# A 32-expert layer whose weight stream changes from 2 MB to 4 MB transfers, and what that does to the matrix engine's reads

## The chip, the cores and the metric

One core of one Trainium2 chip runs the whole program. The time is the device time of one execution in microseconds. The kernel before took 1160.23 us (median of 3 runs, 1159.47 to 1162.91). The profiled execution took 1164.89 us, of which 1163.1 us lie between its first and its last instruction (its span).

## The reference, cut to what matters

A decoder layer on 256 tokens of width 1024, all in float32: a norm, one input projection, a sparse-attention group and a delta-rule group, an output projection with residual, then a norm and a mixture of 32 experts of which each token uses 4. The change lies in the experts:

```python
def expert_ffn(xb, wg, bg, wu, bu, wd, bd):
    gate = jnp.minimum(xb @ wg + bg, SWIGLU_LIMIT)
    up = jnp.clip(xb @ wu + bu, -SWIGLU_LIMIT, SWIGLU_LIMIT)
    glu = gate * jax.nn.sigmoid(gate * SWIGLU_ALPHA)
    return ((up + 1.0) * glu) @ wd + bd
...
top_val, top_idx = lax.top_k(h @ w_router + b_router, 4)
gates = jax.nn.softmax(top_val, axis=-1)
# every expert is applied to the tokens that chose it, weighted by its gate, summed over experts
```

Each expert has three 1024 x 1024 matrices (gate, up, down) of 4 MB; the 96 matrices are 402.7 MB, and all of them are read once.

## The kernel before, in words

The front (attention, delta rule, router) takes about the first 233 us. The rest is a loop over 16 pairs of experts in `pair`, which every engine has its own version of. Up to 64 tokens (`CAP`) are gathered per expert by a matmul with a selection matrix (L928), turned (L937), multiplied with gate and up (`stream`, L964), put through the SwiGLU on the vector and scalar engines (L1765 to L1774), turned (L992), multiplied with down (L964 again), and each pair's result is scattered back onto the tokens by a matmul (L1004) and added to `x` (L1786). Because only 64 rows are live, two matmuls that write the two halves of PSUM's partitions (columns 0 to 511 and 512 to 1023 of the result) stand side by side; each program matmul is two instructions in the trace.

Weights arrive in halves of a matrix. A half is 2 MB, 16 KB in each of 128 partitions, and fills one of ten slots (`SLOTS`). Half `j` goes to slot `EXPERT_RING[j % 10]`; the order of the ring is that in which the front gives the slots up. Half `h` of a matrix holds the rows `h*512 + 4*p + c` in partition `p` (L408), so that four neighbouring rows are one run of memory. SyncE issues them in order in `chunks` (L497 to L502): it waits until the slot's previous half has been used (`freed`), then starts the DMA, whose end raises `landed`. TensorE waits for `landed` in front of each half and raises `freed` behind it. The last half comes in four pieces (`last_chunk`, L504) so that work on it can begin early.

Since row `4*p + c` sits in partition `p`, the other operand has to be in the same order. ACT (L1248) and POOL (L1386) therefore write the normalised tokens `h2` column by column in that order (`rows_of_runs`, `place_of_runs`), and DVE writes `m_act` so (L1774).

In the text below, "the first half of the up matrix of a pair's second expert" is the half with `j % 12 == 8`, since a pair of experts has 12 halves.

Of the kernel before, what the change touches and what calls it, by code (L numbers as in the profile page):

```python
# [24 lines left out]
ALU = mybir.AluOpType  # L25
AX = mybir.AxisListType

P = 128
# [7 lines left out]
NE = 32  # L36
CAP = 64
ROUNDS = SEQ // CAP
FRONT_SLOTS = 4
SLOTS = 10  # L40
PAIRS = NE // 2
BODY = 5
LAPS = 6
TURNS = (PAIRS - 1) // BODY
CHUNKS = 12
# [5 lines left out]
C_ID = 0  # L51
C_IO = C_ID + P
C_ONE = C_IO + CAP
# [41 lines left out]
REGIONS = {"qk_turned": 4, "attention": 5, "inverse": 6, "scan": 7, "turned_input": 8, "tables": 9}  # L95


EXPERT_RING = [3, 0, 4, 5, 7, 1, 6, 2, 8, 9]
assert len(EXPERT_RING) == SLOTS and CHUNKS * BODY == SLOTS * LAPS and 1 + BODY * TURNS == PAIRS

# [76 lines left out]
def hybrid_block(nc, a, out):  # L177
    slab, front_uses, front_landed = slab_plan()
# [8 lines left out]
    with ctx:  # L187
        def sb(name, cols, dt=F32):
            return ctx.enter_context(nc.sbuf_tensor(name, [P, cols], dt))
# [13 lines left out]
        nsa = sb("nsa", 8192 + 2048)  # L203
        rB = nsa[:, 8192:]
        late = {8: nsa[:, 6144:]}

        tables = sb("tables", C_ONE + 4096)
        late[9] = tables[:, C_ONE:]
        cst = tables[:, 0:C_END]
# [7 lines left out]
        def at(name, lo, n):  # L217
            return ring[:, REGIONS[name] * 4096 + lo:REGIONS[name] * 4096 + lo + n]

# [14 lines left out]

        ident = cst[:, C_ID:C_ID + P]
# [122 lines left out]
        def ringv(s):  # L358
            return late[s] if s in late else ring[:, s * 4096:(s + 1) * 4096]

# [23 lines left out]
        def chunk(r, turn, j):  # L384

            k = j % SLOTS
            s = EXPERT_RING[k]
            lap = r * ((6 * NE + SLOTS - 1 - k) // SLOTS) + turn * LAPS + j // SLOTS  # L390
            return s, lap + front_uses[s], lap * 16 + (front_landed[s] + 16)

        def used(eng, r, turn, j):
# [13 lines left out]

        wexp = [a[n][0].rearrange("e (h p c) f -> e h p (c f)", h=2, p=P)  # L408
                for n in ("exp_w_gate", "exp_w_up", "exp_w_down")]

        def rows_of_runs(v):
            return v.rearrange("p (h q c) -> p h c q", h=2, c=4)

# [7 lines left out]
        def _(sp):  # L421
# [34 lines left out]
            sp.dma_start(xt[:, 1, :], xi[1]).then_inc(sem("x1_landed"), 16)  # L456
            sp.dma_start(cst[:, 0:C_ONE], a["const_table"][:, 0:C_ONE]).then_inc(sem("ident_landed"), 16)
            load("c")
# [38 lines left out]

            def chunks(r, turn, lo, hi):
                for j in range(lo, hi):
                    s, uses, _ = chunk(r, turn, j)  # L500
                    sp.wait_ge(freed[s], uses)
                    sp.dma_start(ringv(s), wexp[j % 6 // 2][turn * (2 * BODY) + j // 6, j % 2]).then_inc(landed[s], 16)  # L502

            def last_chunk():  # L504

                s, uses, _ = chunk(0, TURNS - 1, CHUNKS * (BODY + 1) - 1)
                sp.wait_ge(freed[s], uses)
                for c in range(4):
                    sp.dma_start(ringv(s)[:, 1024 * c:1024 * c + 1024], wexp[2][NE - 1, 1][:, 1024 * c:1024 * c + 1024])\
                        .then_inc(landed[s] if c == 3 else sem(f"piece_landed{c}"), 16)  # L510
# [27 lines left out]
        def _(pe):  # L538
# [393 lines left out]
            def turn_rows(m, first=False):  # L932
# [5 lines left out]
                i.then_inc(sem("rows_turned"), 1)  # L938

            def biases(buf):  # L940

                for fh in range(2):
                    for w, o in enumerate((bG, bU)):
                        rows = slice(NE * (w + 1), NE * (w + 2))
                        pe.matmul(o[64 * fh:64 * fh + 64, :], m_eb[buf][rows, :], btab[rows, 512 * fh:512 * fh + 512],  # L945
                                  start=True, stop=False, skip_group_check=True)

            def stream(o, r, turn, j0, lhs, opens=False, pieces=False):

                for j in (j0, j0 + 1):  # L950
                    s, _, val = chunk(r, turn, j)
                    apart = pieces and j > j0
                    if not apart:
                        pe.wait_ge(landed[s], val)
                    w = ringv(s).rearrange("p (c f) -> p c f", c=4)
                    for c in range(4):
                        if apart and c < 3:
                            pe.wait_ge(sem(f"piece_landed{c}"), 16)
                        elif apart:
                            pe.wait_ge(landed[s], val)  # L960
                        cc = (j - j0) * 4 + c
                        lt = lhs[:, (cc % 4) * P + (cc // 4) * CAP:(cc % 4) * P + (cc // 4) * CAP + CAP]
                        for fh in range(2):
                            i = pe.matmul(o[64 * fh:64 * fh + 64, :], lt, w[:, c, 512 * fh:512 * fh + 512],  # L964
                                          start=(opens and cc == 0), stop=(cc == 7), skip_group_check=True)
                            if fh == 1 and c == 3:
                                i.then_inc(freed[s], 1)
                return i

            def pair(r, turn, i, opens=False, last=False):  # L970
                it = r * PAIRS + turn * BODY + i
                j0 = CHUNKS * i
                for par in range(2):
# [5 lines left out]
                    for w, o in enumerate((bG, bU)):  # L979
                        stream(o, r, turn, j0 + 6 * par + 2 * w, m_hT[par])  # L980
                    gather(1 - par, m + 1)
# [409 lines left out]
        def _(dve):  # L1391
            nchain = [0]
            V = nc.vector
# [345 lines left out]

            iota = cst[:, C_IO:C_IO + CAP]  # L1740

            def select(buf, e):

                for t in range(T2):
                    ins = V.tensor_scalar(m_sel[buf][:, t, :], iota, posm[:, t, bass.ds(e, 1)], None, ALU.is_equal)  # L1745
                ins.then_inc(sem("sel_ready"), 1)
                V.tensor_tensor(m_eb[buf], bcast(cst[:, bass.ds(e + (C_ID + NE), 1)], [P, CAP]),
                                bcast(cst[:, bass.ds(e + (C_ID + 2 * NE), 1)], [P, CAP]), ALU.add)\
                    .then_inc(sem("eb_ready"), 1)
# [119 lines left out]
```

## Time and profile before

| | |
|---|---|
| median of 3 runs | 1160.23 us (1159.47 to 1162.91) |
| profiled execution | 1164.89 us, span 1163.1 us |
| TensorE busy | 1089.6 us, 94% |
| VectorE, ScalarE, GpSimd busy | 321.6, 213.2, 38.9 us |
| DMA moved | 430.93 MB in 46585 packets |
| DMA, from 262 us to 1134 us | 425 to 429 GB/s in every slice |
| mean granted TensorE clock | 0.988 |

The page cuts the span into 40 slices of 29 us and gives each engine's busy share in tenths, the granted clock, and what the DMA engines moved. A long busy time says that an engine is used, not that it sets the end: the chain of work that ended last, and who waits for whom, tell that.

### The profile page before, as it was taken

Reading aid. Unit: us, or ns where it says so; the run is one execution under the profiler, and the core shown is the slowest. Engines: PE = TensorE matmul, PEld = TensorE weight load, DVE = VectorE, ACT = ScalarE, POOL = GpSimd, SP = SyncE. Lnnn points to the kernel's source line nnn. Section 1 sums busy time; section 2 is a strip of 40 time slices with the busy share of each in tenths; the row PEclk is TensorE's granted clock in tenths of the full one; section 3 lists DMA queues with packets and bytes.
Section 4 is the critical chain, followed back from the end, with each engine's and each line's share of the span. In section 5 each row is a group of like instructions: output and inputs, shape, how many; then the busy total and the mean of one; then the engine's idle time right before and its main releaser. Section 6 shows DMA issues by size and latency. Waiting matters only on the chain.

```text
span 1163.1 us, 12735 instructions
## 1 busy us (share of the span) xinstructions
PE 1089.6 (94%) x5122; PEld 447.1 (38%) x5122; DVE 321.6 (28%) x660; ACT 213.2 (18%) x410; POOL 38.9 (3%) x43
## 2 busy tenths in 40 slices
PE   6999999899999999999899999989898999999986
PEld 4577587533333333333233333323232333333332
DVE  2377745321212222121212221212121212121221
ACT  3246753311111110101011101110101010101010
POOL 0001240100000000000000000000000000000000
PEclk9999999879999999999999999999999999999999
DMA  9724245779999999999999999999999999999994
GB/s 330 254 89 128 91 163 191 298 288 428 428 426 429 426 429 428 428 426 429 425 428 428 427 427 428 427 428 428 427 429 428 428 427 429 428 427 428 428 426 162
DMA packets 46585, 430.93 MB, mean 371 GB/s; under 512 B 7556, under 2 KB 13148, under 8 KB 22076
## 3 DMA queue, kind: packets, MB, share of 16 engines
q1 hardware_dynamic: 46524, 430.06, 89.2%
q8 instruction: 45, 0.74, 0.3%
q14 instruction: 16, 0.13, 0.0%
HBM read 429.00 MB, written 1.05 MB: 370 GB/s over the span
## 4 chain that ended last, share of the span: by engine, by line
PE 65%; DMA 24%; DVE 4%; ACT 3%; issue 2%; SPq 1%; DVEq 0%; ACTq 0%
PE bank L964 42%; DMA ring<-in_exp_w_up_dram 15%; DMA tables<-in_exp_w_up_dram 8%; PE bank L1004 3%; PE bank L584 3%; PE bank L571 3%; PE bank L601 3%; ACT nsa L1046 3%; PE bank L841 2%; PE bank L945 2%; PE bank L928 2%; DVE nsa L1774 1%; PE bank L592 1%; DVE nsa L1770 1%; PE bank L992 1%
## 5 line engine op out<-in xcount | busy, mean ns | idle before, releaser
L964 PE MATMUL bank<-ring,nsa 128*64 128x512 f32 x2464 | 547.7, 598 | 19.7 <-DMA ring<-in_exp_w_up_dram 9.9
L964 PEld LDWEIGHTS bank<-ring,nsa 128*64 128x64 f32 x2464 | 172.5, 138 | 376.5 <-issue 339.0
L1046 ACT ACTIVATE nsa<-bank 128x512 f32<-128x512 f32 (+6 forms) x187 | 95.2, 543 | 506.3 <-PE bank L928 254.0
L1779 DVE COPY nsa<-bank 64x512 f32<-64x512 f32 x32 | 22.2, 694 | 273.9 <-PE bank L964 273.9
L1765 DVE TENSOR_SCALAR nsa<-bank 128x512 f32<-128x512 f32 x32 | 22.1, 692 | 239.3 <-PE bank L964 239.3
L1043 ACT ACTIVATE nsa<-nsa 128x512 f32<-128x512 f32 (+2 forms) x35 | 21.1, 607 | 345.5 <-DVE nsa L1765 345.5
L964 PE MATMUL bank<-nsa 128*64 128x512 f32 x304 | 69.2, 597 | 3.9 <-DMA nsa<-in_exp_w_up_dram 2.5
L964 PE MATMUL bank<-tables,nsa 128*64 128x512 f32 x304 | 68.6, 593 | 3.6 <-DMA tables<-in_exp_w_up_dram 2.5
L1004 PE MATMUL bank<-nsa 128*128 128x512 f32 x128 | 59.5, 604 | 12.5 <-ACT nsa L1046 12.5
L1770 DVE TENSOR_SCALAR nsa<-bank 128x512 f32<-128x512 f32 x32 | 22.1, 692 | 170.7 <-PE bank L964 170.7
L928 PE MATMUL bank<-rA,nsa 128*64 128x512 f32 x264 | 64.0, 607 | 0.9 <-DVE nsa L1745 0.9
L1786 DVE TENSOR_TENSOR x<-x,bank 128x512 f32<-128x512 f32 x64 | 44.0, 688 | 31.7 <-PE bank L1004 25.3
L571 PE MATMUL bank<-ring,nsa 128*128 128x512 f32 (+1 forms) x128 | 50.0, 547 | 0.0
L584 PE MATMUL bank<-nsa,ring 128*128 128x256 f32 x192 | 42.4, 379 | 0.0
L1004 PEld LDWEIGHTS bank<-nsa 128*128 128x128 f32 x128 | 22.8, 189 | 49.9 <-issue 49.9
L964 PEld LDWEIGHTS bank<-tables,nsa 128*64 128x64 f32 x304 | 21.6, 137 | 48.0 <-issue 41.1
L964 PEld LDWEIGHTS bank<-nsa 128*64 128x64 f32 x304 | 20.8, 137 | 47.3 <-issue 40.2
L945 PE MATMUL bank<-btab,nsa 32*64 32x512 f32 x256 | 35.8, 629 | 3.1 <-issue 3.1
L584 PEld LDWEIGHTS bank<-nsa,ring 128*128 128x128 f32 x192 | 36.2, 190 | 5.2 <-issue 0.5
L1046 ACT ACTIVATE ring<-bank 128x512 f32<-128x512 f32 (+3 forms) x54 | 29.8, 589 | 40.7 <-PE bank L601 15.4
L1774 DVE SCALAR_TENSOR_TENSOR nsa<-nsa 128x512 f32<-128x512 f32 x32 | 33.9, 1058 | 3.3
L928 PEld LDWEIGHTS bank<-rA,nsa 128*64 128x64 f32 x264 | 19.2, 139 | 38.8 <-issue 38.8
(196 smaller groups left out, 650.6 us busy)
## 6 DMA issues: line engine op xcount, KB each, us to landing
ring<-in_exp_w_gate_dram SPq DMA_DIRECT2D x52, 2048.0 KB, 36.2
ring<-in_exp_w_down_dram SPq DMA_DIRECT2D x51, 2048.0 KB, 34.7
ring<-in_exp_w_up_dram SPq DMA_DIRECT2D x50, 2048.0 KB, 36.9
nsa<-in_exp_w_up_dram SPq DMA_DIRECT2D x7, 2048.0 KB, 35.5
tables<-in_exp_w_up_dram SPq DMA_DIRECT2D x7, 2048.0 KB, 37.0
ring<-in_w_in_dram SPq DMA_DIRECT2D x6, 2048.0 KB, 11.6
nsa<-in_exp_w_gate_dram SPq DMA_DIRECT2D x6, 2048.0 KB, 37.8
tables<-in_exp_w_gate_dram SPq DMA_DIRECT2D x6, 2048.0 KB, 39.3
```

Of the source, the lines that this page charges most:

```text
L571: m = pe.matmul(o[:, 0:n], hT[:, c, t * P:(t + 1) * P], w[:, c, 0:n], start=(c == 0), stop=(c == KC - 1))
L584: m = pe.matmul(o[:, u * SEQ:(u + 1) * SEQ], w[:, c, mc0:mc0 + P], hT[:, c, :], start=(c == 0), stop=(c == KC - 1))
L601: m = pe.matmul(o[:, hd * P:(hd + 1) * P], lhs[i][:, hd, :], rhs[i][:, hd, :], start=(i == 0), stop=(i == n - 1))
L841: m = pe.matmul(o[:, :], mixT[:, lo + k, t * P:(t + 1) * P], w[:, k, n * 512:(n + 1) * 512], start=(k == 0), stop=(k == 3))
L928: i = pe.matmul(bA[64 * hf:64 * hf + 64, :], m_sel[buf][:, t, :], h2[:, t, 512 * hf:512 * hf + 512], start=(t == 0), stop=(t == 1), skip_g ...
L945: pe.matmul(o[64 * fh:64 * fh + 64, :], m_eb[buf][rows, :], btab[rows, 512 * fh:512 * fh + 512], start=True, stop=False, skip_group_check= ...
L964: i = pe.matmul(o[64 * fh:64 * fh + 64, :], lt, w[:, c, 512 * fh:512 * fh + 512], start=(opens and cc == 0), stop=(cc == 7), skip_group_ch ...
L1004: i = pe.matmul(scatter_bank[hf][t][:, :], m_selwT[:, t, :], m_y[:, 512 * hf:512 * hf + 512], start=True, stop=not opens)
L1046: return nc.scalar.activation(o, i, ACT.Copy)
L1770: V.tensor_scalar(m_uc, bU[:, :], -7.0, 7.0, ALU.max, ALU.min).then_inc(sem("up_read"), 1)
L1774: V.scalar_tensor_tensor(out=m_act.rearrange("p (c q) -> p q c", c=4), in0=m_uc.rearrange("p (q c) -> p q c", c=4), scalar=1.0, in1=m_gs.r ...
L1786: V.tensor_tensor(xs, xs, scatter_bank[hf][t][:, :], ALU.add).then_inc(sem("added"), 1)
```

## The change

The memory layout of a matrix in SBUF changes: partition `p` now holds the rows `8*p` to `8*p + 7`, which are one run of 32 KB, and half `h` of the matrix is rows `8*p + 4*h + c`. From half 24 on, a matrix is fetched by one DMA into two slots, which for that are laid side by side in SBUF (`PLACE` puts the ring's slots in ring order, slots 8 and 9 both lie in `nsa` now). The first 24 halves (4 experts) and the last 6 (the last expert) still come one by one, the very last in four pieces. The DMA waits until the second of its two slots is free; TensorE waits for the whole matrix in front of its first half and not again in front of its second.

For the down matrix to find its rows in that order, the columns of gate and up are taken in the same order: the matmul that made columns 0 to 511 now makes those whose number has `(n // 4) % 2 == 0`, the other one the rest. It reads runs of 4 floats, 8 floats apart (`in_runs`). The bias rows are read likewise. The constants that the expert loop needs (identity, counting row) move to a buffer of their own, `marks`.

```diff
-        wexp = [a[n][0].rearrange("e (h p c) f -> e h p (c f)", h=2, p=P)
+        wexp = [a[n][0].rearrange("e (p h c) f -> e h p (c f)", h=2, p=P)
...
+        whole = [a[n][0].rearrange("e (p r) f -> e p (r f)", p=P) for n in ("exp_w_gate", "exp_w_up", "exp_w_down")]
...
-            return v.rearrange("p (h q c) -> p h c q", h=2, c=4)
+            return v.rearrange("p (q h c) -> p h c q", h=2, c=4)
...
+            def chunks(r, turn, lo, hi):
+                for j in range(lo, hi, 2):
+                    s, uses, _ = chunk(r, turn, j + 1)
+                    sp.wait_ge(freed[s], uses)
+                    s = chunk(r, turn, j)[0]
+                    sp.dma_start(pairv(s), whole[j % 6 // 2][turn * (2 * BODY) + j // 6]).then_inc(landed[s], 16)
...
-            chunks(0, 0, 0, CHUNKS)
-            with sp.Fori(0, TURNS - 1) as turn:
+            halves(0, 0, 0, SINGLY)
+            chunks(0, 0, SINGLY, CHUNKS * (BODY + 1))
+            for turn in range(1, TURNS - 1):
                 chunks(0, turn, CHUNKS, CHUNKS * (BODY + 1))
-            chunks(0, TURNS - 1, CHUNKS, CHUNKS * (BODY + 1) - 1)
+            chunks(0, TURNS - 1, CHUNKS, CHUNKS * (BODY + 1) - 6)
+            halves(0, TURNS - 1, CHUNKS * (BODY + 1) - 6, CHUNKS * (BODY + 1) - 1)
...
+            def in_runs(w, fh):
+                return w.rearrange("p (q h c) -> p h q c", h=2, c=4)[:, fh]
...
-                    if not apart:
+                    if j == j0:
                         pe.wait_ge(landed[s], val)
+                    elif j < SINGLY or pieces and not apart:
+                        pe.wait_ge(landed[s], second_half(j))
...
-                            i = pe.matmul(o[64 * fh:64 * fh + 64, :], lt, w[:, c, 512 * fh:512 * fh + 512],
+                            wc = w[:, c, 512 * fh:512 * fh + 512] if o is bD else in_runs(w[:, c, :], fh)
+                            i = pe.matmul(o[64 * fh:64 * fh + 64, :], lt, wc,
```

(`halves` is the old `chunks`.) On SyncE, where the fifth expert's weights begin (half 24), the order before is this; 128x4096 is a half, and the ISA rows compute register values of the loop:

```order
L502 DMA ring<-in_exp_w_down_dram 128x4096 x2
L502 ISA
L502 DMA ring<-in_exp_w_gate_dram 128x4096
L502 ISA
L502 DMA ring<-in_exp_w_gate_dram 128x4096
L502 DMA ring<-in_exp_w_up_dram 128x4096 x2
L502 DMA nsa<-in_exp_w_down_dram 128x4096
L502 DMA tables<-in_exp_w_down_dram 128x4096
```

The same place of the change, 128x8192 being a whole matrix:

```order
L518 DMA ring<-in_exp_w_down_dram 128x4096 x2
L527 DMA ring<-in_exp_w_gate_dram 128x8192
L527 DMA ring<-in_exp_w_up_dram 128x8192
L527 DMA nsa<-in_exp_w_down_dram 128x8192
L527 DMA ring<-in_exp_w_gate_dram 128x8192
```

Two DMAs became one, and nothing changed its place among the matrices. The end of the stream, where the last expert begins, stands so before:

```order
L502 DMA ring<-in_exp_w_down_dram 128x4096 x2
L502 DMA ring<-in_exp_w_gate_dram 128x4096 x2
L502 DMA nsa<-in_exp_w_up_dram 128x4096
L502 DMA tables<-in_exp_w_up_dram 128x4096
L502 DMA ring<-in_exp_w_down_dram 128x4096
L509 DMA ring<-in_exp_w_down_dram 128x1024 x4
```

and so after:

```order
L527 DMA ring<-in_exp_w_down_dram 128x8192
L518 DMA ring<-in_exp_w_gate_dram 128x4096 x2
L518 DMA nsa<-in_exp_w_up_dram 128x4096 x2
L518 DMA ring<-in_exp_w_down_dram 128x4096
L534 DMA ring<-in_exp_w_down_dram 128x1024 x4
```

Here only the down matrix of expert 30 is joined; the last six halves stand as they did. The rows of TensorE, VectorE, ScalarE and GpSimd keep their kind, number and place; only source lines and buffer names differ.

## Rows read from the trace of the kernel before

**Rows 1.** The page: TensorE's busy time, and GB/s of the 40 slices.
```profile
PE 1089.6 (94%) x5122; PEld 447.1 (38%) x5122; DVE 321.6 (28%) x660; ACT 213.2 (18%) x410; POOL 38.9 (3%) x43
...
GB/s 330 254 89 128 91 163 191 298 288 428 428 426 429 426 429 428 428 426 429 425 428 428 427 427 428 427 428 428 427 429 428 428 427 429 428 427 428 428 426 162
```
**Rows 2.** Windows: busy us (count) of PE, PEld, DVE, ACT, POOL; clock; DMA share; GB/s.
```profile
300.00:400.00 100.00, 97.78 (x464) 33.55 (x462) 20.08 (x39) 11.59 (x21) 0.00 (x0) 1.00 1.01 428
...
1000.00:1100.00 100.00, 91.73 (x422) 30.10 (x420) 20.84 (x41) 9.59 (x17) 0.00 (x0) 1.00 1.01 428
```
**Rows 3.** The chain that ended last, 296 to 353 us: start, us, what.
```profile
297.11 1.02 PE bank L945 x8
298.13 13.88 PE bank L964 x64
...
352.20 1.00 PE bank L945 x5
```
**Rows 4.** The same chain, 560 us to the end.
```profile
782.91 3.68 PE bank L964 x16
...
1092.22 45.62 DMA tables<-in_exp_w_up_dram
...
1137.88 3.68 PE bank L964 x16
...
1156.41 0.69 DVE x L1786
```
**Rows 5.** Waits: engine, line, waited for: us in total, times, longest.
```profile
SPq L502 <- PE bank L964: 785.0, 181, 13.8
...
PEld bank L964 <- DMA ring<-in_exp_w_up_dram: 19.4, 15, 2.1
```
**Rows 6.** DMA queues (packets, MB, share): 900:1100, 135:139, 22:24, 91:94 us.
```profile
DMA packets 5870, 85.54 MB, mean 428 GB/s; under 512 B 649, under 2 KB 649, under 8 KB 649
...
q1 hardware_dynamic: 5863, 85.43, 100.4%
...
q8 instruction: 7, 0.11, 0.2%
...
q1 hardware_dynamic: 406, 1.66, 101.2%
...
q1 hardware_dynamic: 379, 0.78, 105.4%
...
q1 hardware_dynamic: 1070, 1.10, 108.6%
```
**Rows 7.** The half issued between 310 and 313 us (half 25): KB, us to landing.
```profile
ring<-in_exp_w_gate_dram SPq DMA_DIRECT2D x1, 2048.0 KB, 17.3
```
**Rows 8.** Timeline, 220 to 252 us: start, us, instruction, idle before and releaser.
```profile
221.50 1.06 ACT L1043 ACTIVATE rA<-x 128x1024 f32<-128x1024 f32 x1 [1.05 <-DVE x L1685]
...
224.26 0.29 DVE L1705 TENSOR_TENSOR_SCAN st<-tables,st 128x32 f32<-128x32 f32 x1
...
225.72 2.12 ACT L1248 ACTIVATE rA<-x,st 128x1024 f32<-128x1024 f32 x1 [0.30 <-DVE st L1419]
...
227.99 2.87 POOL L1386 TENSOR_TENSOR rA<-rA,nsa 128x1024 f32<-128x1024 f32 x1 [4.14 <-ACT rA L1248]
...
228.40 2.54 DVE L1705 TENSOR_TENSOR_SCAN st<-tables,st 128x32 f32<-128x32 f32 x1
```
**Rows 9.** The page's costliest groups: busy us, mean ns | idle before, releaser.
```profile
L964 PE MATMUL bank<-ring,nsa 128*64 128x512 f32 x2464 | 547.7, 598 | 19.7 <-DMA ring<-in_exp_w_up_dram 9.9
...
L1765 DVE TENSOR_SCALAR nsa<-bank 128x512 f32<-128x512 f32 x32 | 22.1, 692 | 239.3 <-PE bank L964 239.3
...
L1774 DVE SCALAR_TENSOR_TENSOR nsa<-nsa 128x512 f32<-128x512 f32 x32 | 33.9, 1058 | 3.3
```
**Rows 10.** Timeline, 568 to 592 us: TensorE at the loop's turn.
```profile
575.64 1.24 PE L945 MATMUL bank<-btab,nsa 32*64 32x512 f32 x8 [3.06 <-issue]
```
**Rows 11.** Windows, 576 to 580 us, columns as in Rows 2.
```profile
576.00:580.00 4.00, 4.00 (x16) 1.01 (x10) 0.00 (x0) 0.00 (x0) 0.00 (x0) 0.57 1.01 426
```

More of the change, by code:

```diff
@@ L43 @@
 LAPS = 6
+SINGLY = 24
 TURNS = (PAIRS - 1) // BODY
@@ L98 @@
 EXPERT_RING = [3, 0, 4, 5, 7, 1, 6, 2, 8, 9]
+PLACE = {s: k for k, s in enumerate(EXPERT_RING[:8])}
 assert len(EXPERT_RING) == SLOTS and CHUNKS * BODY == SLOTS * LAPS and 1 + BODY * TURNS == PAIRS
@@ L202, in hybrid_block @@
         rA = sb("rA", 2048)
[L203 to L208, printed above, removed]
+        nsa = sb("nsa", 8192 + 2048 + 4096)
+        rB = nsa[:, 8192:10240]
+        late = {8: nsa[:, 6144:10240], 9: nsa[:, 10240:]}
+        marks = sb("marks", C_ONE)
+        tables = nsa[:, 10240 - C_ONE:]
         cst = tables[:, 0:C_END]
@@ L217, in at @@
         def at(name, lo, n):
-            return ring[:, REGIONS[name] * 4096 + lo:REGIONS[name] * 4096 + lo + n]
+            return ring[:, PLACE[REGIONS[name]] * 4096 + lo:PLACE[REGIONS[name]] * 4096 + lo + n]
         rD = at("qk_turned", 0, 3072)
@@ L233, in hybrid_block @@
         gain2 = nsa[:, 0:1024]
-        ident = cst[:, C_ID:C_ID + P]
+        ident = marks[:, C_ID:C_ID + P]
         ones = cst[:, C_ONE:C_ONE + P]
@@ L358, in ringv, with pairv @@
         def ringv(s):
-            return late[s] if s in late else ring[:, s * 4096:(s + 1) * 4096]
+            return late[s] if s in late else ring[:, PLACE[s] * 4096:(PLACE[s] + 1) * 4096]
+        def pairv(s):
+            return nsa[:, 6144:] if s in late else ring[:, PLACE[s] * 4096:(PLACE[s] + 2) * 4096]
         def signal_of(job):
@@ L391, in chunk, with second_half @@
             return s, lap + front_uses[s], lap * 16 + (front_landed[s] + 16)
+        def second_half(j):
+            k = j % SLOTS
+            s = EXPERT_RING[k]
+            n = j // SLOTS + 1 if j < SINGLY else len([i for i in range(SINGLY) if i % SLOTS == k]) + 1
+            return front_landed[s] + 16 * n
         def used(eng, r, turn, j):
@@ L456, in _ @@
             sp.dma_start(xt[:, 1, :], xi[1]).then_inc(sem("x1_landed"), 16)
-            sp.dma_start(cst[:, 0:C_ONE], a["const_table"][:, 0:C_ONE]).then_inc(sem("ident_landed"), 16)
+            sp.dma_start(marks[:, :], a["const_table"][:, 0:C_ONE]).then_inc(sem("ident_landed"), 16)
             load("c")
@@ L496, in _, with halves @@
             sp.dma_start(gain2, a["ffn_norm_g"][0].partition_broadcast(P)).then_inc(sem("gain2_landed"), 16)
-            def chunks(r, turn, lo, hi):
+            def halves(r, turn, lo, hi):
                 for j in range(lo, hi):
@@ L509, in last_chunk @@
                     sp.dma_start(ringv(s)[:, 1024 * c:1024 * c + 1024], wexp[2][NE - 1, 1][:, 1024 * c:1024 * c + 1024])\
-                        .then_inc(landed[s] if c == 3 else sem(f"piece_landed{c}"), 16)
-            chunks(0, 0, 0, CHUNKS)
-            with sp.Fori(0, TURNS - 1) as turn:
+                        .then_inc(sem(f"piece_landed{c}"), 16)
+            halves(0, 0, 0, SINGLY)
+            chunks(0, 0, SINGLY, CHUNKS * (BODY + 1))
+            for turn in range(1, TURNS - 1):
                 chunks(0, turn, CHUNKS, CHUNKS * (BODY + 1))
-            chunks(0, TURNS - 1, CHUNKS, CHUNKS * (BODY + 1) - 1)
+            chunks(0, TURNS - 1, CHUNKS, CHUNKS * (BODY + 1) - 6)
+            halves(0, TURNS - 1, CHUNKS * (BODY + 1) - 6, CHUNKS * (BODY + 1) - 1)
             last_chunk()
@@ L944, in biases @@
                         rows = slice(NE * (w + 1), NE * (w + 2))
-                        pe.matmul(o[64 * fh:64 * fh + 64, :], m_eb[buf][rows, :], btab[rows, 512 * fh:512 * fh + 512],
+                        pe.matmul(o[64 * fh:64 * fh + 64, :], m_eb[buf][rows, :], in_runs(btab[rows, :], fh),
                                   start=True, stop=False, skip_group_check=True)
@@ L951, in stream @@
                     s, _, val = chunk(r, turn, j)
-                    apart = pieces and j > j0
-                    if not apart:
+                    apart = pieces and j == CHUNKS * (BODY + 1) - 1
+                    if j == j0:
                         pe.wait_ge(landed[s], val)
+                    elif j < SINGLY or pieces and not apart:
+                        pe.wait_ge(landed[s], second_half(j))
                     w = ringv(s).rearrange("p (c f) -> p c f", c=4)
                     for c in range(4):
-                        if apart and c < 3:
+                        if apart:
                             pe.wait_ge(sem(f"piece_landed{c}"), 16)
-                        elif apart:
-                            pe.wait_ge(landed[s], val)
                         cc = (j - j0) * 4 + c
@@ L979, in pair @@
                     for w, o in enumerate((bG, bU)):
-                        stream(o, r, turn, j0 + 6 * par + 2 * w, m_hT[par])
+                        stream(o, r, turn, j0 + 6 * par + 2 * w, m_hT[par], pieces=(last and par == 1))
                     gather(1 - par, m + 1)
@@ L1738, in _ @@
                                         scalar=1.0, in1=chosen, op0=ALU.add, op1=ALU.mult))
-            iota = cst[:, C_IO:C_IO + CAP]
+            iota = marks[:, C_IO:C_IO + CAP]
             def select(buf, e):
@@ L1746, in select @@
                 ins.then_inc(sem("sel_ready"), 1)
-                V.tensor_tensor(m_eb[buf], bcast(cst[:, bass.ds(e + (C_ID + NE), 1)], [P, CAP]),
-                                bcast(cst[:, bass.ds(e + (C_ID + 2 * NE), 1)], [P, CAP]), ALU.add)\
+                V.tensor_tensor(m_eb[buf], bcast(marks[:, bass.ds(e + (C_ID + NE), 1)], [P, CAP]),
+                                bcast(marks[:, bass.ds(e + (C_ID + 2 * NE), 1)], [P, CAP]), ALU.add)\
                     .then_inc(sem("eb_ready"), 1)
```

## The prediction

> **What bounds the kernel now.** I read the page first. TensorE is busy for 94% of the span, which makes it look like the bound, but GB/s stands at 425 to 429 in thirty slices in a row, from about 260 us almost to the end [rows 1]. Two things that are both nearly full need a second view. The windows say which one has room: the DMA share is 1.01 early and late, while TensorE's busy time falls from 97.78 to 91.73 us in 100 [rows 2]. TensorE has gaps, the DMA engines have none.
>
> The chain of waits says the same in periods. Early, one pair of experts follows the last after 352.20 - 297.11 = 55.09 us without any DMA in the chain [rows 3]: that is what TensorE and its helpers need by themselves. Late, the chain passes through the landing of the last half of a pair's up matrices; six pairs take 1137.88 - 782.91 = 354.97 us, 59.16 us each [rows 4], or 4.93 us per half. Without the weights TensorE would be done at 297.11 + 15 x 55.09 + 3.1 (the turn of its loop, [rows 10]) + 6.7 (from 1156.41 to the end of the span, [rows 4]) = 1133.3 us, 30 us ahead of the real end. SyncE's long waits for TensorE [rows 5] are no contradiction: ten slots are full of transfers that are under way (45.62 us from issue to landing late in the run, [rows 4]), so nine halves queue in front of the engines. So the time is the start of the stream, plus 402.7 MB at the stream's rate, plus some 25 us of work after the last landings. Only the stream's rate, its start and that tail can move the end.
>
> **The change: packets.** The DMA engines handle a run of memory as one packet. Between 900 and 1100 us, 85.43 MB are 5214 packets of 16 KB; the other 649 are the tiny ones that tell a semaphore, one to eight packets of data [rows 6]. A full queue gives the time of a packet as engine time over packets, 16 engines times the stretch: 1 KB packets (91 to 94 us) 48/1070 = 44.9 ns, 2 KB (22 to 24 us) 32/379 = 84.4 ns, 4 KB (135 to 139 us) 64/406 = 157.6 ns, and 16 KB (3200 - 8.7)/5214 = 612.1 ns, where 8.7 us are charged to the small packets and the code fetch [rows 6]. Were all of it bytes, four times 157.6 would be 630. The line from the 4 KB row to 16 KB has 37.9 ns per KB and leaves 6.1 ns that do not depend on size; from the 2 KB row it is 9.0, from the 1 KB row 7.1. I take 7.1, the middle one, and keep 6.1 and 9.0.
>
> Halves 24 to 185 come as 81 whole matrices. Each saves, on every engine, eight packets of data and one small one: 9 x 7.1 = 64 ns, and 81 x 64 ns = 5.2 us (4.4 to 6.6). A 32 KB packet is in no row; below, the saving is bounded by nothing at all (a packet cut back to 16 KB), above by the nearest rows' 9.0 ns.
>
> The DMA page of the Trainium skill (DMA: Bandwidth & Descriptors, Why small descriptors are slow) speaks against this size: it puts a fixed cost of about 3 cycles beside one per 32 bytes on each packet, which is 0.6% of 16 KB. By that estimate halving the packets saves 0.3% of 81 matrices, 2.3 us, and not 5.2. The 16 KB and 4 KB rows show more than that per packet, so my sum goes by them.
>
> **The change: waits.** A joint DMA starts when its second slot is free, one half later than its first half did. That matters only if the queue runs dry. At its thinnest, where the joint ones begin, half 25 was issued behind half 24 and landed after 17.3 us [rows 7]; two halves of 4.93 leave 7.4 us that were ahead of both. The joint DMA goes out at that same moment, so the queue stays full: cost nothing. If it did run dry, every us of it would be lost.
>
> TensorE now waits for whole matrices. Per pair of experts it has about 59.16 - 0.38 - 55.09 = 3.7 us to spare; before, this came in small waits (longest 2.1 us, [rows 5]), now most of it falls together in front of one up matrix. In the middle the stream hides that. What counts is the last one, half 176 of expert 29: from its landing TensorE needs 55.09 us to the same place of the next pair, and one half (13.88/4 = 3.47 us, [rows 3]) until it stands before half 189. The stream needs 12 halves less four joint savings, 59.16 - 0.26 = 58.9 us. 58.6 against 58.9: just hidden, with 0.3 us left where there were over three before. I charge 0.3 us for it. After 189 nothing changes: halves 190 and 191 come singly and in pieces as they did.
>
> **The change: reading in runs.** Of each expert, 64 instructions of gate and up (13.88 us, [rows 3]) and the bias rows now read 4 floats and skip 4. No row shows TensorE reading like that. The nearest are of other engines: ACT takes 1.06 us over 1024 neighbouring floats and 2.12 us when it reads every fourth one [rows 8]; on DVE the step that writes its columns far apart takes 1058 ns beside 692 [rows 9]. Below I set no gain, since the columns are as many; above stand the factors 1.53 and 2.0. I take no cost, because those rows touch one float in each 16 bytes and this read uses every float of the 16 bytes it touches, as the contiguous read does.
>
> The skill has a rule for that (Advanced Engine Details and Errata, SBUF Cachelines): lines of 16 bytes, full speed from two hits on a line. With four hits it would be free, so the rule's sum is mine; by the ACT row's factor alone it would be hundreds of us. The ACT row agrees with the rule's other half.
>
> A small slowing would be hidden anyhow: gate and up are 32 x 13.88 = 444 us, TensorE's own end lies 1158.2 - 1133.3 = 24.9 us before the new one (1158.2 comes out of the sum below), and 24.9/444 is 5.6%.
>
> **The change: the rest.** In the front, ACT L1248 and POOL L1386 read every eighth float instead of every fourth. They already pay for a new 16 bytes with each float; I take no cost, at most once more their 2.12 and 2.87 us, which would reach the expert loop's start because DVE's scan beside POOL took 2.54 instead of 0.29 us [rows 8]. The unrolled loop on SyncE, `marks` and the new places of slots cost nothing: SyncE only waits.
>
> **Sum.** 5.2 - 0.3 = 4.9 us off the stream's end: the profiled execution's 1164.89 becomes 1160.0, its span 1158.2. The median of the runs lies 4.66 us below the profiled time, so 1160.23 - 4.9 = 1155.3 us.
>
> **Rivals.**
> 1. *Bytes, not packets, set the rate.* If the constant is a property of small packets only, or if 32 KB runs are cut back to 16 KB, what is left is at most the small packets, 81 x 7.1 ns = 0.6 us, less the 0.3: 1159.9. For it: the step from 1 KB to 2 KB to 4 KB to 16 KB isn't quite straight (39.5, 36.6, 37.9 ns per KB out of the four numbers above). Against it: three rows give 6 to 9 ns. The skill's 3 cycles would land between, at 1158.2.
> 2. *Skipping reads slow the matmuls* (the slower side). From 5.6% on, TensorE sets the end and each further percent costs 4.4 us. With DVE's 1.53: 0.53 x 444 - 24.9 = 210 us, 1366; with 10%, 19.5 us, 1175. For it: ACT's and DVE's rows. Against it: every 16 bytes are still used whole.
> 3. *The pooled wait drops the clock.* After 3.06 us without work at the loop's turn [rows 10], the granted clock over the next 4 us was 0.57, so part of it ran at 1.2 GHz instead of 2.4 [rows 11]. Waits of about 3 us now come once a pair. In the middle this is hidden (1.5 us against 3.7); in front of half 189 it isn't: 1.5 us minus what is already charged, about 1156.5.
> 4. *The stream speeds up more,* each KB at the 36.6 ns between the 2 KB and 4 KB rows: 16 KB in 586 instead of 606 ns is 3.4% of 81 matrices (81 x 9.86 = 799 us), 27 us. With the 5.2 that is more than TensorE can follow, and the end goes to TensorE's own, 29.8 us sooner: 1130.4. For it there is only that one pair of rows.
>
> **How the numbers follow.** What a measurement of this kernel tells from no change is about 0.3%, 3.5 us: faster means below 1156.75. Forecast (5.2 us minus at most about 2 of the tail): 0.58, of it 0.50 faster and 0.08 same. Rival 1: 0.15, 0.13 same. Rival 3: 0.10, half and half. Rival 2: 0.13, slower. Rival 4: 0.04. Together faster 0.61, same 0.26, slower 0.13. The range takes in the forecast with 6.6 us saved and some us of luck in the rate, and rival 1 with a us of spread: 1151 to 1161. Rivals 2 and 4 are left out.
>
> **What would show it.** Right: 81 x 16 x 9 = 11,664 packets fewer than 46585, GB/s at 430 to 431 in the full slices, six pairs at 58.8 us each, waits for up matrices of about 3 us, the same mean for L964's matmuls (598 ns), DVE's and POOL's rows of the front unchanged. Packets at 16 KB or GB/s at 428 mean rival 1; a longer L964 and a period above 58.8 without DMA in the chain mean rival 2; a mean clock under 0.98 means rival 3. Holes in GB/s after 310 us would mean that the late start of joint DMAs, which I set at nothing, is what counts.

## The result and the profile after

The changed kernel takes 1155.17 us (median of 5 runs, 1153.3 to 1158.5), the one before 1161.03 us (5 runs, 1159.47 to 1162.91). The ratio is 0.9938, 95% interval 0.9922 to 0.9955: 0.6% faster. The forecast was 1155.3.

The page after, against [rows 1]: the busy time of each engine, GB/s of the 40 slices, and the packets of the whole run.

```profile
PE 1087.9 (94%) x5122; PEld 450.3 (39%) x5122; DVE 321.7 (28%) x660; ACT 212.9 (18%) x410; POOL 38.9 (3%) x43
...
GB/s 334 255 90 124 96 165 177 289 336 430 434 426 435 433 427 432 433 430 427 434 430 428 432 434 430 429 432 430 430 432 431 430 430 434 429 430 432 434 419 161
DMA packets 34919, 430.91 MB, mean 374 GB/s; under 512 B 6260, under 2 KB 11852, under 8 KB 20780
```

The full slices moved from about 428 to about 431 GB/s. There are 46585 - 34919 = 11,666 packets fewer. No engine's busy time moved by more than 3.2 us. The same two windows as [rows 2] (busy us of PE, PEld, DVE, ACT, POOL; clock; DMA share; GB/s):

```profile
300.00:400.00 100.00, 97.15 (x462) 33.12 (x456) 20.66 (x40) 12.16 (x22) 0.00 (x0) 1.00 1.01 432
1000.00:1100.00 100.00, 92.78 (x430) 31.61 (x430) 22.36 (x46) 10.21 (x18) 0.00 (x0) 1.00 1.00 430
```

The DMA engines are still full and TensorE still has gaps late in the run: the bound is the same and has moved a little. The queue from 900 to 1100 us, against [rows 6]:

```profile
DMA packets 2959, 86.12 MB, mean 431 GB/s; under 512 B 328, under 2 KB 328, under 8 KB 328
...
q1 hardware_dynamic: 2953, 86.02, 100.0%
```

86.02 MB in 2953 - 328 = 2625 packets are 32 KB each: the long runs are kept whole. The costliest group, against [rows 9] (busy us, mean ns | idle before):

```profile
L996 PE MATMUL bank<-ring,nsa 128*64 128x512 f32 x2464 | 544.4, 597 | 15.9 <-DMA ring<-in_exp_w_up_dram 8.1
```

L996 is the line that was L964. Its matmuls, two thirds of which now read in runs of four floats, take 597 ns where they took 598. The early chain against [rows 3] (start, us, what):

```profile
293.70 1.02 PE bank L976 x8
294.72 13.88 PE bank L996 x64
...
348.80 1.02 PE bank L976 x8
```

The period is 348.80 - 293.70 = 55.10 us, against 55.09 before. The late chain, against [rows 4]:

```profile
735.91 39.34 DMA ring<-in_exp_w_up_dram
...
1027.44 40.73 DMA ring<-in_exp_w_up_dram
...
1068.22 7.11 PE bank L996 x32
...
1085.74 42.34 DMA nsa<-in_exp_w_up_dram
1128.12 3.68 PE bank L996 x16
...
1142.94 3.69 PE bank L1036 x8
1146.65 0.69 DVE x L1818
```

From the landing at 735.91 + 39.34 = 775.25 to the one at 1027.44 + 40.73 = 1068.17 are five pairs: 58.58 us each. The same five pairs of the kernel before end with this landing, at 1078.10, and start at 782.87, which is 59.05 us each:

```profile
1033.48 44.62 DMA ring<-in_exp_w_up_dram
```

The sixth pair, up to half 189, takes longer in both, 59.91 and 59.74 us, so that six pairs take 58.80 us each where there were 59.16. TensorE now starts a whole matrix (x32) behind the landing, and only at the end, behind half 189, half of one (x16) as before.

**Which part of the difference is the change.** The two profiled executions differ by 1163.1 - 1153.4 = 9.7 us, the medians by 5.9. SyncE's rows show a part of it that has nothing to do with the change. They show the issue of half 10, the first DMA that waits for the expert loop; first of the kernel before, then of the changed one:

```profile
246.72 3.76 SPq L502 DMA_DIRECT2D ring<-in_exp_w_down_dram  x2
```

```profile
243.32 3.76 SPq L518 DMA_DIRECT2D ring<-in_exp_w_down_dram  x2
```

3.4 of the 9.7 us were there before the first joint DMA. Windows of TensorE around that time, before and then after:

```profile
238.00:242.00 4.00, 4.00 (x16) 1.35 (x17) 0.00 (x0) 1.88 (x2) 0.00 (x0) 0.50 0.33 139
242.00:246.00 4.00, 4.00 (x12) 1.09 (x10) 0.00 (x0) 0.00 (x0) 0.00 (x0) 0.58 0.00 0
```

```profile
234.00:238.00 4.00, 3.33 (x8) 0.53 (x4) 1.78 (x8) 0.60 (x1) 0.00 (x0) 0.60 0.91 360
238.00:242.00 4.00, 3.98 (x24) 1.54 (x26) 0.00 (x0) 1.88 (x2) 0.00 (x0) 1.00 0.31 131
```

TensorE ran at 1.2 GHz until about 245 us in the one execution and until about 237 us in the other, so the expert loop's first matmuls were slow in one and not in the other. E10 below shows that this moves between executions of one program. So I compare profiled executions from the issue of half 10 on. From there to the landing of half 189 the kernel before takes 1137.84 - 246.72 = 891.12 us and the changed one 1128.08 - 243.32 = 884.76: 6.4 us less. That, and not 9.7, is the change.

### The profile page after: what moved, and what is told of

It is laid out like the page before. It is cut to its first block, busy times and chain, and to the rows that moved or that the text cites. A ratio compares the mean times of both kernels' runs of the same rounds, so it can differ in the third digit from the quotient of the medians.

```text
span 1153.4 us, 12445 instructions
## 1 busy us (share of the span) xinstructions
PE 1087.9 (94%) x5122; PEld 450.3 (39%) x5122; DVE 321.7 (28%) x660; ACT 212.9 (18%) x410; POOL 38.9 (3%) x43
## 2 busy tenths in 40 slices
DMA packets 34919, 430.91 MB, mean 374 GB/s; under 512 B 6260, under 2 KB 11852, under 8 KB 20780
## 3 DMA queue, kind: packets, MB, share of 16 engines
HBM read 429.00 MB, written 1.05 MB: 373 GB/s over the span
## 4 chain that ended last, share of the span: by engine, by line
PE 68%; DMA 22%; DVE 5%; ACT 3%; issue 1%; SPq 0%; DVEq 0%; ACTq 0%
PE bank L996 44%; DMA ring<-in_exp_w_up_dram 14%; DMA nsa<-in_exp_w_up_dram 7%; PE bank L598 4%; PE bank L1036 3%; PE bank L611 3%; PE bank L628 3%; ACT nsa L1078 2%; PE bank L868 2%; PE bank L976 2%; PE bank L955 2%; DVE nsa L1806 1%; PE bank L619 1%; PE bank L1024 1%; DVE nsa L1802 1%
## 5 line engine op out<-in xcount | busy, mean ns | idle before, releaser
L996 PE MATMUL bank<-ring,nsa 128*64 128x512 f32 x2464 | 544.4, 597 | 15.9 <-DMA ring<-in_exp_w_up_dram 8.1
L996 PEld LDWEIGHTS bank<-ring,nsa 128*64 128x64 f32 x2464 | 174.3, 137 | 367.6 <-issue 345.5
L996 PE MATMUL bank<-nsa 128*64 128x512 f32 x608 | 136.3, 601 | 4.9 <-DMA nsa<-in_exp_w_up_dram 3.5
L996 PEld LDWEIGHTS bank<-nsa 128*64 128x64 f32 x608 | 42.8, 138 | 93.1 <-issue 84.6
L1036 PE MATMUL bank<-nsa 128*128 128x512 f32 x128 | 59.5, 604 | 12.5 <-ACT nsa L1078 12.5
L1036 PEld LDWEIGHTS bank<-nsa 128*128 128x128 f32 x128 | 22.7, 189 | 49.9 <-issue 49.9
L1078 ACT ACTIVATE ring<-bank 128x512 f32<-128x512 f32 (+3 forms) x54 | 29.8, 589 | 39.8 <-PE bank L628 15.4
L598 PEld LDWEIGHTS bank<-ring,nsa 128*128 128x128 f32 x128 | 24.8, 197 | 23.1 <-issue 21.0
```

The lines of the kernel that those rows point to most:

```text
L598: m = pe.matmul(o[:, 0:n], hT[:, c, t * P:(t + 1) * P], w[:, c, 0:n], start=(c == 0), stop=(c == KC - 1))
L996: i = pe.matmul(o[64 * fh:64 * fh + 64, :], lt, wc, start=(opens and cc == 0), stop=(cc == 7), skip_group_check=True)
L1036: i = pe.matmul(scatter_bank[hf][t][:, :], m_selwT[:, t, :], m_y[:, 512 * hf:512 * hf + 512], start=True, stop=not opens)
L1078: return nc.scalar.activation(o, i, ACT.Copy)
```

## The experiments

Each ratio is to the kernel before, in runs of the same chip. "Stream" is the time from the issue of half 10 to the landing of half 189, "to the end" that from the same issue to the start of the last group of matmuls of L1004 or L1036 (before: 1152.70 - 246.72 = 905.98; after: 1142.94 - 243.32 = 899.62). The row of before:

```profile
1152.70 3.69 PE bank L1004 x8
```

**E1, the runs alone.** The new split of the rows and the reads in runs, in the kernel before; halves still come singly.

```diff
-        wexp = [a[n][0].rearrange("e (h p c) f -> e h p (c f)", h=2, p=P)
+        wexp = [a[n][0].rearrange("e (p h c) f -> e h p (c f)", h=2, p=P)
...
+            wc = w[:, c, 512 * fh:512 * fh + 512] if o is bD else in_runs(w[:, c, :], fh)
```

> The kernel before with the new layout alone: halves in order (p h c), gate, up and bias rows read in runs of 4 floats, every half still fetched by its own DMA (16 KB packets, 2 MB). Packet theory (each packet costs about 7 ns beside its bytes): nothing in the stream changes, so the time is that of before within 1.5 us (about 1161), and 16 KB packets stay at about 612 ns of engine time. Rival A, the skipping read costs TensorE something: L964's matmuls above 598 ns and a pair period above 55.09 us in the part that TensorE sets. Rival B, the layout itself (memory order, 32 KB between partitions) makes the stream faster: about 1155, GB/s above 428.

Measured: 1163.75 us (12 runs) against 1162.93 (23), ratio 1.0005 (0.9993 to 1.0016); stream 890.97. The reads in runs cost nothing: its chain has the row below, the same to 0.01 us as the contiguous read.

```profile
923.40 13.88 PE bank L969 x64
```

**E2, joint DMAs of 16 KB runs.** The changed kernel, slots, pooled waits, unrolled loop and all, but with the old split of the rows, so that one DMA brings two runs of 16 KB per partition; reads are contiguous.

```diff
-    whole = [a[n][0].rearrange("e (p r) f -> e p (r f)", p=P) ...
+    whole = [a[n][0].rearrange("e (h p r) f -> e p h (r f)", h=2, p=P) ...
-    sp.dma_start(pairv(s), whole[...][...])
+    sp.dma_start(pairv(s).rearrange("p (h r) -> p h r", h=2), whole[...][...])
```

> The changed kernel with the old order of rows and contiguous column reads: whole matrices by one DMA into two neighbouring slots, but as two runs of 16 KB in each partition. Same waits and same number of DMAs as the changed kernel, packets as before (about 46,600 less 81 x 16 small ones). Packet theory: only the small packets go, 0.6 us, minus 0.3 us of tail, so about 1160.5, the time of before within 1.5 us. Rival C, joint DMAs as such (fewer issues and completions) bring the gain: about 1155. Rival D, whole-matrix waits cost something that the changed kernel's packets hide: above 1162.5.

Measured: 1162.75 us (12 runs), ratio 1.0008 (0.9995 to 1.002); stream 891.53. Its queue between 900 and 1100 us:

```profile
DMA packets 5548, 85.53 MB, mean 428 GB/s; under 512 B 328, under 2 KB 328, under 8 KB 328
```

As many small packets as in the changed kernel (328), but data in 16 KB packets and the old rate. So fewer DMAs, fewer semaphore packets and fewer waits are worth nothing; the gain is in the length of the runs. Rival 1's remnant, 0.6 us from small packets, isn't there either: from 320 to 1100 us E2 moves 332.98 MB with 1272 small packets, the kernel before 333.00 MB with 2540.

**E3, runs of 8 KB.** The kernel before with each half brought by two DMAs.

```diff
-   sp.dma_start(ringv(s), wexp[...][...]).then_inc(landed[s], 16)
+   for u in range(2):
+       sp.dma_start(ringv(s)[:, 2048 * u:2048 * u + 2048],
+                    wexp[...][...][:, 2048 * u:2048 * u + 2048]).then_inc(landed[s], 16)
```

> The kernel before with every half fetched by two DMAs of 8 KB runs (1 MB each) instead of one of 16 KB runs; waits as before. This doubles the suspected cost. Packet theory: per half and engine 8 more data packets and 1 more small one, 9 x 7.1 = 64 ns, for the 180 halves from half 10 on 11.5 us: 1172.5 (6.1 ns: 1171, 9.0 ns: 1175.6), GB/s about 423. Rival 1 of the prediction (bytes alone set the rate at these sizes): at most 180 x 7 ns = 1.3 us, about 1162.

Measured: 1175.06 us (4 runs), ratio 1.0103 (1.0084 to 1.0122): 12 us slower, the mirror of the change and larger: 180 halves by 8 are 1440 more data packets, where the change took away 648. Its stream takes 904.40 us, 13.28 more than before, or 9.2 ns for each. The queue from 320 to 1100 us of before, of the changed kernel, and of E3:

```profile
q1 hardware_dynamic: 22864, 333.00, 100.4%
```

```profile
q1 hardware_dynamic: 11514, 335.35, 100.0%
```

```profile
q1 hardware_dynamic: 45025, 327.86, 101.1%
```

780 us by 16 engines are 12,480 us. Over the data packets, by their megabytes 40,022, 20,325 and 10,234, that is 311.8 ns for 8 KB, 614.0 ns for 16 KB and 1219.5 ns for 32 KB, the small packets' share included. Two of 8 KB cost 9.6 ns more than one of 16 KB, two of 16 KB 8.6 ns more than one of 32 KB.

**E4 and E5, extra matmuls before the expert loop.** The late rise of the clock costs some 3 us, so I tried to keep TensorE busy in the router's wait: two more matmuls in E4, six smaller ones (32 rows instead of 128) in E5, some of them around the gather (their results are overwritten by the work that follows).

```diff
+            def keep_busy(n):
+                for _ in range(n):
+                    pe.matmul(bS1[:, :], ident, gain2[:, 0:512], start=True, stop=True)
...
+            keep_busy(2)
```

> The changed kernel with two extra matmuls (128x512, results never used, into a free bank) placed where TensorE waits for the router's choice, just ahead of the expert loop. In the profile of before the clock was granted at half for 20.5 us around the loop's start, in that of after for 13.7 us, and half 10 (the start of the stream) was issued 3.4 us earlier in the latter. Clock theory: with TensorE kept busy the half-clock stretch ends sooner, half 10 goes out up to 3 us before the changed kernel's 243.3 us, and the time falls by as much: 1152 to 1154. Rival: the stretch is set by what went before, nothing changes, or the extra matmuls delay the gather: 1155 to 1158.

> The changed kernel with six extra matmuls (results never used): three in the wait for the router's choice, one before the gather, one after it, one after the turn, all ahead of the expert loop. Two such matmuls (e4) changed nothing in the clock. Clock theory: with the gaps around the gather filled too, full clock comes back before 240 us, half 10 goes out before 243 us, and the time is 1150 to 1153. Rival: they only delay the gather by 1 to 3 us and the stretch stays, 1156 to 1160.

Measured: E4 1156.45 us (6 runs), ratio 0.9942 (0.9922 to 0.9963), no different from the change itself. E5 1160.24 us (12 runs), ratio 0.9979 (0.9966 to 0.9992), worse by some 4 us than the change. E4's matmuls filled only the router's wait, and the clock stayed low until about 245 us. E5 left TensorE no gap from 226 us on, and the clock still came back only for part of the time around 240 us, fell again, and half 10 went out at 248.42 us, later than in any other profiled execution. Windows of E4, then of E5:

```profile
238.00:242.00 4.00, 4.00 (x14) 0.77 (x8) 0.00 (x0) 1.68 (x2) 0.00 (x0) 0.50 0.00 0
242.00:246.00 4.00, 4.00 (x14) 1.22 (x12) 0.00 (x0) 0.00 (x0) 0.00 (x0) 0.63 0.00 0
```

```profile
234.00:238.00 4.00, 4.00 (x8) 1.12 (x10) 2.85 (x14) 0.00 (x0) 0.00 (x0) 0.50 0.77 262
238.00:242.00 4.00, 4.00 (x12) 1.00 (x8) 0.00 (x0) 1.47 (x3) 0.00 (x0) 0.85 0.61 262
242.00:246.00 4.00, 4.00 (x15) 0.97 (x16) 0.00 (x0) 1.01 (x1) 0.00 (x0) 0.58 0.00 0
```

My theory of a cheap warming fell in both forms. Behind the loop's start E5 is the change: its stream takes 884.68 us.

**E6 and E7, reads with real strides.** To see what TensorE pays for skipping when the 16 bytes are not used whole. Gate and up read other floats of the same slots, so that the output is not the layer's: E6 one float in each 32 bytes, E7 every second float.

```diff
-  wc = ... else in_runs(w[:, c, :], fh)
+  wc = ... else ringv(s).rearrange("p (q k) -> p k q", k=8)[:, 2 * c + fh]      # E6
+  wc = ... else w[:, c, :].rearrange("p (q h) -> p h q", h=2)[:, fh]            # E7
```

> The changed kernel, but gate and up read every eighth float of the slot (one float in each 32 bytes, 512 columns as before; it reads parts of the slot that belong to other columns, so the output is not the layer's). This is the read that ACT's row of before paid double for. Theory (what counts is how much of each 16 bytes is used, which is nothing for TensorE at four floats of four): L996's mean rises from 598 ns, by up to a factor of 2 for gate and up, TensorE then sets the end at 1155 + up to 420 us. Rival: TensorE doesn't mind any stride of float32 columns, time as after, about 1156.

> The changed kernel, but gate and up read every second float of a row (two floats in each 16 bytes; columns go to other places, so the output is not the layer's). If one float in 32 bytes costs TensorE something and two in 16 bytes nothing, a full-speed limit lies between; if e6 costs nothing, neither does this: about 1156 us, L996 at 598 ns. If the cost goes by 16-byte pieces per column, it lies at half of e6's.

Measured, one run each: E6 1637.86 us, E7 1161.18. The 64 matmuls of gate and up in E6's chain and in E7's:

```profile
325.21 29.51 PE bank L997 x64
```

```profile
297.73 14.55 PE bank L997 x64
```

Runs of four floats 13.88, every second float 14.55 (1.05 times), lone floats 29.51 (2.13 times). Every second float adds 32 x 0.67 = 21.4 us, more than all of the room: E7's late chain has no DMA in it, TensorE sets its end, and from the issue of half 10 (245.07) to the last group of matmuls it takes 903.81 us, 4.2 more than the changed kernel. The start of that group:

```profile
1148.88 3.69 PE bank L1037 x8
```

E6 is bound by TensorE alone; its DMA share falls to 0.72 in the late window:

```profile
1000.00:1100.00 100.00, 97.99 (x304) 23.86 (x302) 13.97 (x26) 7.77 (x14) 0.00 (x0) 1.00 0.72 289
```

**E8, joint from half 12.** `SINGLY = 12` in place of 24: six more matrices come whole, where the queue is thin.

> The changed kernel with whole matrices from half 12 on instead of 24. Packets theory: six more matrices save 6 x 64 ns = 0.4 us. Dry-queue theory: at half 12 the queue is thin (halves 12 and 13 landed 12.4 us after issue, two of them are 9.9 us, so 2.5 us are left in front of the joint one, less the fixed part of a landing), so the stream shows a hole or two of up to 2 us between 250 and 310 us, and the time from half 10's issue to the landing of half 189 is that of after (884.8 us) plus 0 to 4 us.

Measured, one run: 1161.05 us; to the end 1148.84 - 246.72 = 902.12, 2.5 us more than the changed kernel. Its windows, and then the same ones of the changed kernel:

```profile
256.00:262.00 6.00, 5.78 (x32) 2.33 (x30) 1.74 (x2) 1.96 (x4) 0.00 (x0) 1.00 1.03 399
...
268.00:274.00 6.00, 6.00 (x32) 1.97 (x30) 0.11 (x1) 0.00 (x1) 0.00 (x0) 1.00 0.92 333
```

```profile
256.00:262.00 6.00, 5.77 (x30) 2.19 (x30) 0.00 (x0) 1.30 (x3) 0.00 (x0) 1.00 1.00 429
...
268.00:274.00 6.00, 6.00 (x32) 2.00 (x30) 1.71 (x5) 0.63 (x1) 0.00 (x0) 1.00 1.01 431
```

Two holes: some 6 x 30/429 + 6 x 98/431 = 1.8 us of stream lost, more than six matrices save. The last pooled up matrix lands still later, at 1036.31 + 39.20 = 1075.51 us, which is 828.79 us behind half 10 where the changed kernel has 824.85: 3.94 us more, of which the holes explain less than half. The rest is open, with one execution to go by. Of the 3.94 us the changed kernel's waits behind that landing (0.50 and 0.94 us, shown below) cover 1.44, and the other 2.5 come out at the end.

**E9, joint to the end.** The last expert's gate and up come whole too, and TensorE waits for each whole matrix.

```diff
-  chunks(0, TURNS - 1, CHUNKS, CHUNKS * (BODY + 1) - 6)
-  halves(0, TURNS - 1, CHUNKS * (BODY + 1) - 6, CHUNKS * (BODY + 1) - 1)
+  chunks(0, TURNS - 1, CHUNKS, CHUNKS * (BODY + 1) - 2)
+  halves(0, TURNS - 1, CHUNKS * (BODY + 1) - 2, CHUNKS * (BODY + 1) - 1)
...
-  stream(o, r, turn, j0 + 6 * par + 2 * w, m_hT[par], pieces=(last and par == 1))
+  stream(o, r, turn, j0 + 6 * par + 2 * w, m_hT[par])
```

> The last expert's gate and up come jointly too; only its down halves are still fetched singly, at the very end. It saves two more matrices' worth of packets (2 x 64 ns by my price), but the last joint pair makes TensorE wait for an up half that lands with its partner, near the end of the stream where there is little slack: some 3.5 us of idle moved behind the stream, of which about 0.5 to 1 us is covered. My theory: 2 to 4 us slower than the change as it stands, about 1158.5, ratio to before 0.996 to 0.998. Rival (the waits of pooled transfers are hidden wherever they stand): no difference, ratio 0.994, and the last chain ends on the stream again.

Measured: 1160.68 us (12 runs), ratio 0.9984 (0.997 to 0.9997), 3.4 us above E10 on the same chip. The chain's end, and the window behind the last landing:

```profile
1085.42 42.20 DMA nsa<-in_exp_w_up_dram
1127.66 8.80 PE bank L996 x32
```

```profile
1128.00:1132.00 4.00, 4.00 (x14) 1.02 (x12) 0.00 (x0) 0.00 (x0) 0.00 (x0) 0.61 0.71 295
```

The stream ends as early as ever, but 32 matmuls instead of 16 now stand behind it, and they run partly at 1.2 GHz (8.80 us instead of 7.11). To the end: 1147.59 - 243.12 = 904.47, 4.85 us more. It is 3.4 us of matmuls more and 1.7 us of clock, less 0.3.

**E10, the changed kernel once more.** Unaltered, for the scatter. (The stream had gained 6.4 us; the 8 us in the expectation is a slip.)

> The changed kernel once more, unaltered, for the scatter of its own start. Theory (8 us of stream time less by fewer packets, the same in every execution): ratio 0.994 to 0.996, and from the issue of half 10 to the landing of half 189 again 884.5 to 885.0 us, while the issue itself falls anywhere from 243 to 247 us. Rival (part of the gain was one lucky start): ratio 0.997 or nearer to 1.

Measured: 1157.29 us (8 runs, 1153.09 to 1158.94) against 1162.76 (19), ratio 0.9946 (0.9928 to 0.9965). It issued half 10 at 246.39 us, 3.1 us later than the first profile of the same program. The last pooled wait but one, in the first profile of the changed kernel and in E10 (idle before it in brackets):

```profile
1068.22 7.09 PE L996 MATMUL bank<-ring,nsa 128*64 128x512 f32 x32 [2.54 <-DMA ring<-in_exp_w_up_dram]
```

```profile
1071.28 8.78 PE L996 MATMUL bank<-ring,nsa 128*64 128x512 f32 x32 [2.54 <-DMA ring<-in_exp_w_up_dram]
```

The landing comes 1068.17 - 243.32 = 824.85 and 1071.24 - 246.39 = 824.85 us behind half 10: the stream repeats to the hundredth. After the same wait, TensorE's clock fell in one execution and not in the other. To the end E10 takes 1146.26 - 246.39 = 899.87 us, 0.25 more: TensorE no longer waits for half 189 and is itself last, by a hair. The sum closes: the slow clock costs 8.78 - 7.09 = 1.69 us, and the waits that the changed kernel still has behind this place, 0.50 and 0.94 us, cover 1.44 of it.

## Why the prediction was right, step by step

**What bounds the kernel: right.** E3 and the change move the rate of the stream and the end follows, 12 us up and 6 us down, while TensorE's instructions stay the same. That TensorE had room was right, too, but it is smaller than I had it. Without its 21.4 us of dearer reads E7 would take 903.81 - 21.4 = 882.4 us from half 10 to the end, which leaves 905.98 - 882.4 = 23.6 us of room in the kernel before, where my 1133.3 gave 29.8, and 17.2 in the changed one, where I had 24.9. The step that I left out stands in the trace of before. In one pair, the first of the loop's last five, the program also adds the bias of the down matrix (L1007), between the matmuls of L1004:

```profile
916.20 1.10 PE bank L1004 x2
917.30 1.05 PE bank L1007 x2
...
924.67 1.02 PE bank L945 x8
```

From 916.20 to 924.67 are 8.47 us where that step takes 3.69, so 4.8 us more. Another 1.7 us is the slow clock behind the loop's turn, which I had as a rival and not in this sum: in E7's chain the stretch behind the turn, from 581.73 to 609.38 us, takes 27.65 us where the same one takes 25.97 in the pair from 296.71 to 322.68. Together they are what was missing. The forecast did not hang on it, the price of rival 2 did.

**The packets: mechanism right, price a little low, and counted on the wrong packets.** I charged 7.1 ns to each of nine packets per engine and matrix. E2 takes away the small one and gains nothing in its ratio, its rate or its stream (891.53 us). So the gain belongs to the eight data packets: 6.36 us / (81 x 8) = 9.8 ns for each by the stream, 8.6 by the windows; from 8 to 16 KB it is 9.6 by the windows and 9.2 by the stream. That is 5.6 to 6.4 us for 81 matrices where I had 5.2; what makes the 0.8 us between stream and windows no run settles. The line through smaller packets gave 6.1 to 9.0; the larger ones lie at its top and a little above. By my estimate from the fixed cost that the Trainium skill states (DMA: Bandwidth & Descriptors, Why small descriptors are slow) the gain would have been 2.3 us; the trace does not agree, at 8.6 to 9.8 ns for each packet.

**The late joint issue at no cost: right.** No slice after 262 us is under 419 before the last, and E8 shows what happens where less is queued: two holes, and 2.5 us at the end.

**The pooled waits: right that they are hidden, 0.3 us too dear.** I expected up to 3.7 us of idle in one place and 0.3 us of slack before half 189. The wait is 2.54 us at 1068.22, and the whole row of the waits is

```profile
PEld bank L996 <- DMA ring<-in_exp_w_up_dram: 12.5, 7, 3.4
```

TensorE then stood idle twice more, 0.94 us of it before half 189, so the tail lost nothing:

```profile
1108.62 7.09 PE L996 MATMUL bank<-ring,nsa 128*64 128x512 f32 x32 [0.50 <-DMA ring<-in_exp_w_down_dram]
...
1128.12 3.65 PE L996 MATMUL bank<-nsa 128*64 128x512 f32 x16 [0.94 <-DMA nsa<-in_exp_w_up_dram]
```

The slack was 1.44 us and not 0.3 because this last period of the stream took 59.91 us, where I had put 58.9; TensorE's own part, 59.91 - 1.44 = 58.5, was as forecast (58.6). Why the stream is slower in that pair (before it took 59.74) no run shows. E9 shows how thin this is: one more pooled wait, at the place without slack, costs over half of the gain.

**Reading in runs at no cost: right,** by the group's mean (597 against 598 ns), by the 13.88 us of 64 matmuls and by E1. The rows of ACT and DVE that I set as upper bounds were of another kind of read: E6 touches one float in each 32 bytes and pays 2.13. The rule of the Trainium skill (Advanced Engine Details and Errata, SBUF Cachelines) that I had followed agrees for runs of four; it takes two hits on a line of 16 bytes to be enough, and E7, which has two, pays 5%.

**The rest at no cost: right in the front.** ACT's and POOL's two steps that now read every eighth float:

```profile
217.84 2.15 ACT L1280 ACTIVATE rA<-x,st 128x1024 f32<-128x1024 f32 x1 [0.30 <-DVE st L1451]
...
220.49 2.88 POOL L1418 TENSOR_TENSOR rA<-rA,nsa 128x1024 f32<-128x1024 f32 x1 [32.24 <-ACT rA L1280]
```

2.15 and 2.88 us, against 2.12 and 2.87 [rows 8].

**The sum:** minus 4.9 predicted; minus 5.9 by the medians (5.5 on E10's chip), minus 6.1 to 6.4 by the two profiles from half 10 on. The two errors, 0.4 to 1.2 us of packets and 0.3 us of tail, have one sign. That the median, 1155.17, lies so close to 1155.3 is luck: the saving was 1.0 us larger than forecast, and the kernel before, at 1161.03, was 0.8 us slower than the 1160.23 that I had counted from.

**The rivals.** 1 is refuted by the 32 KB packets and by E2. 2 is refuted by E1; its threshold of 5.6% was too high: E7's 21.4 us, 4.8% of 444, already cost 4.2 us at the end, so 17.2/444 = 3.9% is where TensorE takes over. 3 does happen: at 833.56 us of the changed kernel, where it is hidden, and at 1071.28 us of E10, where it costs 0.25 us and not the 1.2 I had, because 1.44 us of slack stood behind it. Over many runs the mean clock shows it: 0.987 to 0.991 in E1's twelve, without pooled waits, 0.981 to 0.987 in E2's twelve, with them. The row at 833.56 and its window:

```profile
833.56 8.78 PE L996 MATMUL bank<-nsa 128*64 128x512 f32 x32 [2.54 <-DMA nsa<-in_exp_w_up_dram]
```

```profile
836.00:840.00 4.00, 4.00 (x16) 1.27 (x14) 0.00 (x0) 0.00 (x0) 0.00 (x0) 0.76 0.97 418
```

4 is refuted by the rate, 431 and not 443 GB/s.

What stays open: whether the clock falls after a wait of 2.54 us differs between executions of one program, and no run here says on what it depends. The same holds for the rise of the clock at the loop's start.

## What to carry to other kernels

Where a stream of DMA keeps its engines full, the length of the run is worth a fixed time per packet: price it from the kernel's own small and large packets, charge it to data packets alone, and expect little above 16 KB (0.7% of the rate here). A layout that reads whole runs of 16 bytes lets such a transfer be made without cost to TensorE. Pooling transfers pools waits: leave single transfers where the queue is thin and where no slack is left to cover the wait, at both ends of the stream. Count a loop's unusual passes before you say how much room an engine has: here one pass in sixteen was 4.8 us longer. And before a few us between two profiles are explained, compare them from an event behind the noisy part.

## What the runs showed of the hardware that I had not expected

- A matmul's moving operand of 512 f32 columns takes the same time in runs of four floats as contiguously (13.88 us for 64), 1.05 times as long at every second float, and 2.13 times at one float in 32 bytes.
- In this full stream the DMA queue's packets cost 8.6 to 9.8 ns each beyond their bytes, and this still held from 16 to 32 KB (614.0 and 1219.5 ns). The small packets that tell a semaphore cost nothing that E2 could show (12 runs, 1.0008).
- The stream is far more regular than the rest: 824.85 us in two executions of the same program, whose half 10 went out 3.1 us apart.
- One small DVE step beside POOL's long one is slow, and it is not always the same instruction: before, it was the scan, 2.54 us instead of 0.29, and after it was another one:

```profile
227.96 2.54 DVE L1733 TENSOR_TENSOR st<-st 128x32 f32<-128x32 f32 x1
```
